# Twelve DRAM to DRAM copies of cache rows, begun in the MLP instead of in the delta-rule heads

## The reference, cut to what matters

```
h = rms_norm(x); proj = h @ w_in            # q, k, v, z, a, b | q, k, v of attention | two gates
o_a = gated_delta_rule(q, k, v, ...)        # 4 heads of 128
o_b = dilated_group_attention(...)          # 3 groups x 4 heads of 64, window caches
x = x + (gate_a * (o_a @ w_br_a) + gate_b * (o_b @ w_br_b)) @ w_out
x = x + square(relu(rms_norm(x) @ w_up)) @ w_down
new_win = kv_src[:, -keep:]                 # the caches' new contents are outputs as well
```

## Time and profile before

| | us |
|---|---|
| runs | 2178.13 to 2181.57, median 2179.8 |
| span of the profiled execution | 2175.8 |
| PE busy | 1977.4 (91%) |
| PE weight loads busy | 1913.5 (88%) |
| DVE busy | 733.8 (34%) |
| ACT busy | 635.6 (29%) |
| POOL busy | 564.9 (26%) |

### The profile page before, as it was taken

How to read it: one execution, slowest core, us unless ns; L and a number is a source line. 1 busy time by engine, 2 the same in 40 slices (tenths; PEclk the granted TensorE clock), 3 DMA queues, 4 the chain that set the end, 5 groups by cost and what they waited for, 6 DMA issues and landing times.

```text
span 2175.8 us, 32922 instructions
## 1 busy us (share of the span) xinstructions
PE 1977.4 (91%) x12388; PEld 1913.5 (88%) x12388; DVE 733.8 (34%) x1549; ACT 635.6 (29%) x1390; POOL 564.9 (26%) x334
## 2 busy tenths in 40 slices
PE   5877995997798679999999899999999999999998
PEld 5876895896798679998899899999999999999998
DVE  5523342242243312222221652364135115314513
ACT  7331241332233133333333342322013113202311
POOL 1131122123113011110111353444134214313432
PEclk8898997998998799999999999999999999999999
DMA  4222122122122242344454232311111111111112
GB/s 131 80 75 66 52 95 85 51 77 79 51 90 76 58 134 86 115 130 132 131 150 167 97 126 79 98 40 49 49 49 39 49 49 40 49 49 44 45 59 80
DMA packets 235493, 174.17 MB, mean 80 GB/s; under 512 B 15917, under 2 KB 224890, under 8 KB 235218
## 3 DMA queue, kind: packets, MB, share of 16 engines
q1 hardware_dynamic: 201026, 143.09, 21.7%
q10 hardware_dynamic: 34352, 29.37, 4.0%
HBM read 135.14 MB, written 47.72 MB: 84 GB/s over the span
## 4 chain that ended last, share of the span: by engine, by line
PE 74%; DMA 9%; DVE 8%; ACT 4%; issue 4%; POOL 1%; SPq 0%; ACTq 0%; DVEq 0%; POOLq 0%
PE dense L215 47%; PE dense L240 10%; DMA at_scratch<-at 5%; PE work L1292 2%; PE work L1304 1%; PE work L956 1%; PE work L966 1%; PE work L1342 1%; DVE systems L817 1%; PE work L1325 1%; DVE summed L1644 1%; PE work L1284 1%; PE work L896 1%; DMA sq<-t_scratch 1%; PE work L923 1%
## 5 line engine op out<-in xcount | busy, mean ns | idle before, releaser
L204 POOL TENSOR_TENSOR WL<-Wraw,WH 128x1024 fp32r<-128x1024 f32 (+1 forms) x131 | 312.8, 2388 | 1181.0 <-ACT WH L199 1180.8
L215 PE MATMUL dense<-hH,WH 128*128 128x352 f32 x1464 | 484.0, 331 | 13.7 <-issue 7.4
L215 PE MATMUL dense<-hL,WH 128*128 128x352 f32 x1464 | 477.3, 326 | 0.0
L215 PE MATMUL dense<-hH,WL 128*128 128x352 f32 x1464 | 477.2, 326 | 0.0
L240 PE MATMUL dense<-hH,WH 128*128 128x352 f32 x720 | 267.6, 372 | 61.0 <-ACT fill L249 61.0
L215 PEld LDWEIGHTS dense<-hH,WH 128*128 128x128 f32 x1464 | 281.8, 192 | 16.4 <-issue 11.6
L215 PEld LDWEIGHTS dense<-hL,WH 128*128 128x128 f32 x1464 | 282.3, 193 | 0.0
L215 PEld LDWEIGHTS dense<-hH,WL 128*128 128x128 f32 x1464 | 281.0, 192 | 0.0
L215 PE MATMUL dense<-gH,WH 128*128 128x352 f32 x768 | 248.4, 323 | 4.7 <-issue 2.3
L215 PE MATMUL dense<-gL,WH 128*128 128x352 f32 x768 | 247.7, 323 | 0.0
L215 PE MATMUL dense<-gH,WL 128*128 128x352 f32 x768 | 247.7, 323 | 0.0
(11 more groups left out here) (299 smaller groups left out, 2664.2 us busy)
## 6 DMA issues: line engine op xcount, KB each, us to landing
Wraw<-in_w_in SPq DMA_DIRECT2D x51, 512.0 KB, 4.1
Wraw<-in_w_up SPq DMA_DIRECT2D x32, 512.0 KB, 4.0
Wraw<-in_w_down SPq DMA_DIRECT2D x32, 512.0 KB, 3.5
raw<-qkv_scratch SPq DMA_DIRECT2D x7, 1584.0 KB, 8.3
cache<-in_cache_win SPq DMA_DIRECT2D x20, 512.0 KB, 6.0
qkv_scratch<-fill ACTq DMA_DIRECT2D x54, 176.0 KB, 2.1
gb_scratch<-fill ACTq DMA_DIRECT2D x24, 176.0 KB, 2.1
gates<-ga_scratch SPq DMA_DIRECT2D x8, 528.0 KB, 3.6
```

The source lines that it names most:

```text
L204: G.tensor_tensor(WL[:, s, 0:k], Wraw[:, s, 0:k], WH[:, s, 0:k].bitcast(F32), ALU.subtract).then_inc(sem("w_split"), 1)
L215: ins = PE.matmul(out[:, 0:TN], w[:, s, k0 + k, :], x[:, k, cols], start=(k == 0 and i == 0), stop=(k == nk - 1 and i == 2))
```

## The change

The three copies leave `head_sync` and become the function `cache_rows(sp, q, g)`. In the MLP's loop over q, SP begins group 0 behind the load of block 2 of `w_up`, group 1 behind that of block 4, group 2 behind that of block 6. The sequences are 2q and 2q+1, as they were 2h and 2h+1. The wait on `cache_out` goes from `head_stored` to the end of SP's program. The other engines' programs are unchanged.

```diff
+        def cache_rows(sp, q, g):
+
+            drop = WIN[0] - TSEQ if g == 0 else PAST
+            src, dst = (x[0][bass.ds(2 * q, 2)].rearrange("b t s h d -> b t (s h d)") for x in (a[f"cache_win{g}"], a[f"win{g}_s"]))
+            sp.dma_start(dst[:, 0:drop], src[:, min(WIN[g], PAST) - drop:]).then_inc(sem("cache_out"), 16)
...
             for j in range(6, 8):
                 load(j)
 
-            for g in range(3):
-                drop = WIN[0] - TSEQ if g == 0 else PAST
-                src, dst = (x[0][bass.ds(2 * h, 2)].rearrange("b t s h d -> b t (s h d)") for x in (a[f"cache_win{g}"], a[f"win{g}_s"]))
-                sp.dma_start(dst[:, 0:drop], src[:, min(WIN[g], PAST) - drop:]).then_inc(sem("cache_out"), 16)
             sp.wait_ge(sem("tails_out"), h + 1)
...
             sp.wait_ge(sem("tails_stored"), 96 * NH + 1)
-            sp.wait_ge(sem("cache_out"), 48 * NH)
...
                 for m in range(8):
                     load_cols(sp, N_MLP + m, N_MLP + m + 16 * q, w_up, q * D + m * P)
+                    if m in (2, 4, 6):
+                        cache_rows(sp, q, m // 2 - 1)
...
             for x, (name, before) in enumerate(y_sems):
                 sp.wait_ge(sem(name), before + 16 * len(range(x, NT9, 4)))
+            sp.wait_ge(sem("cache_out"), 48 * 4)
```

## The result

The changed kernel takes 2085.36 us in the median (2082.62 to 2087.19), the kernel before in the same session 2178.97 us (2177.88 to 2181.57): a ratio of 0.957, with a 95% interval of 0.955 to 0.958. The change wins 93.6 us. I had forecast 106.8 us and a range of 2064 to 2092. The profiled execution spans 2082.5 us, 93.3 less than that of before.

What follows compares the result with a forecast made beforehand. The prediction took the kernel as bound by TensorE, winnable where a chain held up by the store of `at`, queued behind copies, leaves it standing or slow: 98.8 (chain) + 8.0 (clock) - 0 (MLP) = 106.8 us, giving 2073.0 us, range 2064 to 2092.

Steps and rivals of the forecast that it cites:

- The bound and its cause: Heads: copies in SP's queue delay the store of `at`; store begin to PE's restart falls from 198.0 to 99.2 us.
- The store's own time: Heads: without copies ahead of it the store of `at` takes 3.5 us, between 3.2 and 4.1.
- The rest of the chain: Heads: from the store's landing to PE's restart at line 945, 21.3 us per head.
- one such collision: Solve in each head: one small DVE step lengthened beside POOL's weight split, 2.14 us in head two.
- The clock: PE's restart after the solve: a 2.8 us pause keeps 2.4 GHz, gaining 2.0 us per head, 8 in four.
- What is late next: Heads: PE's filler ends 22 us after the store begins, the chain at 24.8, leaving 2.8 us idle.
- The MLP: Copies behind `w_up` loads: loads behind big copies land 13 to 16 us after their begin, PE does not stall; cost 0.
- The slack of 24.6 us: MLP: PE stalls only when a weight load lands more than 24.6 us after its begin.
- Rival B: MLP loads behind copies stall PE: 2161 us at 41 us per copy; chance 0.05 with gain left, 0.02 slower.
- The sum: Whole kernel: 98.8 + 8.0 - 0 = 106.8 us gained, span 2069.0 us, time 2073.0 us.
- Rival C: Heads: the store of `at` is slow by itself, not from the copies, so nothing is won: 2180 us; chance 0.02.
- Rival A: Heads: something else comes late, PE restarts at 30 us and low clock, gain 78 us, 2102 us; chance 0.09.

Runs made afterwards that it cites:

- x_pool: Changed kernel with POOL doing two masked levels, then waiting for DVE's solve before job 7's weight split and the third level: 2071.28 us, ratio 0.952.
- e_block: Changed kernel with all three copies of a quarter together behind the third weight load of `w_up`: 2148.34 us, ratio 0.986.
- x_mid: `x_pool` with three of the six filler parts done ahead of PE's transposes and three left between the levels: 2061.85 us, ratio 0.947.
- x_fill: Changed kernel with the six filler parts between the block levels done ahead of PE's transposes of `t_all`: 2074.68 us, ratio 0.953.

## Why the prediction was right, and where it was too large

**The bound and its cause.** Right. Of the 198.0 us from the begins of the stores to PE's restarts, 102.8 are left (25.43, 25.83, 25.80 and 25.75), so 95.2 us were won where I had 98.8. The copies were the cause, shown four ways: the loss is gone without them in the heads (the change), gone when they are spread over 16 engines, three fifths back when 2.1 MB stay, and falls on the next head's first weight load when they stand behind `t_all`.

The Trainium skill, "DMA: Bandwidth & Descriptors", section "Why a DMA increments its semaphore by 16 and not by 1", lets the outermost size choose the number of engines. The runs agree: with 16 in place of 2 the DMA share rose from 0.13 to about 1, and the copies ran at 313 GB/s instead of 52. That rule named a second remedy in a few lines of the kernel, and I had used it only to explain the 13%.

**The store's own time.** 3.5 us assumed, 3.2 measured.

**The rest of the chain.** I took 21.3 us behind the landing; the four heads show 22.2 to 22.6. The step that failed is "I count one such collision". Before, each head's solve has one long step (1.5 to 2.2 us). Now each has two: beside the weight split, as foreseen (2.30 us for a step that takes 0.47), and at the end of POOL's three masked levels, which the earlier solve now meets (1.69 for 0.28). Before, the levels were over long before the solve could start; I had the row for the one and never asked what else POOL does right behind `at`. Behind the landings the four heads take 4.8 us more than I had, the stores 1.2 us less: 3.6 us of the miss.

The Trainium skill's "SBUF — State Buffer", section "SBUF: two separate sides", calls the port pair that DVE and POOL share an exclusive lock, which is held for the whole instruction while the other engine waits; for DVE it names instructions in a 2-port mode, and those with two inputs in SBUF against a POOL instruction that reads SBUF. The long steps agree: in head two they end at 308.92 and 317.48 us, 0.1 and 0.3 us after the POOL instructions that they met (308.78 and 317.17).

**The clock.** The term that failed outright: I had 8 us, and from restart to line 976 the four heads take 86.2 us against 87.4 before, so 1.2 us (2.8 when the changed kernel was run again). I wrote that the clock had held through 3.6 us of idle time, so that a pause of 2.8 us would leave it at 2.4 GHz. What I read was when it fell, not whether a shorter pause prevents the fall. In the changed kernel it fell in every head, in head two 0.4 us before PE began again at 326.99, in the other three 0.1 to 0.9 us after. Stretches of a microsecond in head two, then in head three, where PE begins again at 486.15 (columns as in the earlier trace rows):

```profile
326.00:327.00 1.00, 0.01 (x1) 0.02 (x1) 0.00 (x0) 0.00 (x0) 0.00 (x0) 0.79 1.05 290
327.00:328.00 1.00, 1.00 (x5) 1.00 (x6) 0.00 (x0) 0.00 (x0) 0.00 (x0) 0.50 1.14 337
...
332.00:333.00 1.00, 1.00 (x6) 1.00 (x6) 0.00 (x0) 0.23 (x1) 0.00 (x0) 0.50 0.00 0
333.00:334.00 1.00, 1.00 (x9) 1.00 (x8) 0.00 (x0) 0.36 (x1) 0.00 (x0) 0.80 0.06 16
...
486.00:487.00 1.00, 0.85 (x8) 0.85 (x8) 0.15 (x1) 0.00 (x0) 0.00 (x0) 1.00 1.16 313
487.00:488.00 1.00, 0.67 (x4) 0.35 (x3) 1.00 (x2) 0.00 (x0) 0.00 (x0) 0.50 1.12 353
```

In head two it stayed at 0.50 for nearly 7 us, 6.4 of them behind the restart, where before it was 4.7 in this head; in the other heads for 3.4 us. The size of the term was about right: had the clock stayed in all four heads, as in heads three and four of `x_pool`, they would take 4 x 19.96 = 79.8 us, 7.6 less than before. The step that failed is the condition, that so short a pause keeps the clock. Against heads with the short low stretch the clock is worth 1.6 us a head (`x_pool`).

**What is late next.** Right: PE's filler ended 2.7 to 3.1 us before the chain (2.8 forecast), since the fills come in time. From one head's restart to the next it is 23.2 to 24.0 us less than before, just short of the 24 to 28 forecast.

**The MLP.** Right in mechanism: the loads behind big copies land 13.2 to 17.2 us after their begin, two of the eight a little above the 13 to 16 worked out, PE does not notice, and leaving the copies out changes nothing. The slack of 24.6 us was 3 us too small, on the safe side (`e_block`). Rival B's stall is real as well; the blocked copies reached it.

**The sum.** Terms as measured: 95.2 + 1.2 = 96.4 us, against 93.3 in span. The remaining 3 us lie outside the heads' inner part: the first store begins at 143.27 us instead of 141.05, ahead of any copy, and at 141.56 in the repeated run, so 2 us of them vary from run to run; the last one is not traced. The range held the time, since its upper end had been worked out without the clock's gain. Rival C fell with the result, where the store takes 3.2 us. Rival A came in part: the restart was 1.0 us late and at the low clock, as it says, but not 5 us late.

## What to carry to other kernels

When a small transfer on the critical path takes ten times what its like takes elsewhere, read what was begun before it in the same queue and how many engines that occupies: a copy whose outermost size is 2 runs on two engines, and everything behind it, and the stores of another queue are late with it (ACT's waits for them went from 131.5 us to 7.2). Spread it or move it to where the loads behind it have slack, and work that slack out from the buffers: it must cover what is left of the copies when the load is begun, and the load itself, so one at a time (13 to 17 us here), not three together (42 to 48). When a stall shrinks, check what the freed step now runs beside, and fill the few microseconds in which TensorE still stands: the two together were worth another 20 us here (`x_mid`).

## What the runs showed of the hardware that I had not expected

- The granted clock can fall after a pause that is already over. It did after 1.3 to 1.6 us of standing in two heads of `x_pool` and after 2.7 to 3.1 us in every head of the changed kernel. The fall came 1.8 us after PE's restart in `x_pool`, and between 0.4 us before and 0.9 us after it in the changed kernel; after 0.91 us in the other two heads of `x_pool` it did not, and with the pause filled (`x_fill`, `x_mid`) it stayed at 1.00 through the same transposes.
- A DVE step of 64 x 1 elements took 2.23 us beside a POOL instruction on a 128 x 1024 tile; the step of 64 x 4 right behind it took 0.15 us.
- Two engines copied DRAM to DRAM at 52 GB/s over a head's copies, sixteen at 313, partly beside other transfers: six times as much from eight times the engines.
